# Key norm and output norm of an RWKV-7 group formed per token, two numbers a token, and spread over the channels by products with the unit matrix

## What is computed

```
kk = heads(k * k_k)
kk = kk / max(sqrt(sum(kk * kk, -1)), 1e-12)          # key norm, one number per token and head
...
yc = y - mean(y, -1)
yn = yc * rsqrt(mean(yc * yc, -1) + 64e-5) * g + b    # output norm, one number per token and head
```

## Time and profile before

| | |
|---|---|
| time, median of 3 runs | 4246.4 us (4245.26 to 4247.04) |
| span of the profiled execution | 4199.6 us |
| PE busy, DVE busy, POOL busy | 2858.0, 2419.6, 2387.5 us |
| ACT busy | 671.8 us |
| read from memory over the span | 1310.53 MB, 315 GB/s |

### The profile page before, as it was taken

The page is one execution under the profiler, slowest core; times in us unless marked ns, Lnnn a source line. Parts: engine busy times, 40 slices in busy tenths (PEclk is TensorE's granted clock), DMA queues, the critical chain, the costliest instruction groups (busy, mean ns, idle before and its releaser), DMA issues. The chain is left out here.

```text
span 4199.6 us, 48966 instructions
## 1 busy us (share of the span) xinstructions
PE 2858.0 (68%) x18591; PEld 1580.0 (38%) x18591; DVE 2419.6 (58%) x5633; ACT 671.8 (16%) x1913; POOL 2387.5 (57%) x2194
## 2 busy tenths in 40 slices
PE   7887376787746777768567777667545666675566
PEld 5666354445413343446134343344112222330011
DVE  3427977565864555667855555569745465673311
ACT  3331122220011122101012222101011111000000
POOL 0001366665455665675765665665666776676764
PEclk9988677888977787879788987789767767687788
DMA  3125688889788988899998897998999999999997
GB/s 110 69 67 208 226 303 312 313 332 385 288 324 317 347 289 315 331 374 351 352 371 304 336 339 285 338 374 313 373 378 356 360 383 359 388 373 349 370 365 297
DMA packets 371523, 1325.36 MB, mean 316 GB/s; under 512 B 40188, under 2 KB 75416, under 8 KB 360152
## 3 DMA queue, kind: packets, MB, share of 16 engines
q0 software_dynamic: 314576, 1145.45, 72.7%
q1 hardware_dynamic: 56712, 176.79, 11.2%
HBM read 1310.53 MB, written 11.29 MB: 315 GB/s over the span
## 5 line engine op out<-in xcount | busy, mean ns | idle before, releaser
L752 POOL DMA_INDIRECT ring_u<-in_peer_u,idx x1088 | 1222.6, 1124 | 1088.3 <-DVE gates L1703 396.0
L1460 DVE CUSTOM_DVE_ANT_0 ring_u<-ring_u,h 128x1024 f32<-128x1024 f32 x1088 | 1294.2, 1224 | 568.3 <-DMA ring_u<-in_peer_u,idx 447.3
L752 POOL DMA_INDIRECT ring_v<-in_peer_v,idx_t x1042 | 1114.2, 1069 | 686.5 <-PE pacc L1110 347.9
L1110 PE MATMUL pacc<-ring_v,spread_w 128*32 128x512 f32 x4168 | 1029.2, 737 | 470.6 <-DMA ring_v<-in_peer_v,idx_t 343.0
L1110 PEld LDWEIGHTS pacc<-ring_v,spread_w 128*32 128x32 f32 x4168 | 170.5, 121 | 1050.5 <-DMA ring_v<-in_peer_v,idx_t 686.3
L1085 PE MATMUL pm<-arena 64*64 64x64 f32 (+1 forms) x6256 | 375.8, 257 | 273.8 <-issue 147.1
L1071 PE MATMUL pm<-hT,wts 128*128 128x256 f32 (+2 forms) x2656 | 544.9, 365 | 25.1 <-issue 14.0
L1071 PEld LDWEIGHTS pm<-hT,wts 128*128 128x128 f32 x2656 | 465.0, 208 | 144.6 <-issue 78.0
L1085 PEld LDWEIGHTS pm<-arena 64*64 64x64 f32 x6256 | 295.5, 157 | 434.7 <-issue 251.2
L1071 PE MATMUL pm<-wts,hT 128*128 128x384 f32 (+1 forms) x576 | 201.3, 504 | 7.5 <-DMA wts<-in_sets 7.4
L1071 PE MATMUL pm<-wts,mixT 128*128 128x128 f32 (+1 forms) x1152 | 148.2, 283 | 13.1 <-DVEq L541 5.1
(11 more groups left out here) (223 smaller groups left out, 2708.2 us busy)
## 6 DMA issues: line engine op xcount, KB each, us to landing
wts<-in_sets SPq DMA_DIRECT2D x82, 1536.0 KB
ring_u<-in_peer_u,idx POOLq DMA_INDIRECT x1088
ring_v<-in_peer_v,idx_t POOLq DMA_INDIRECT x1042
wts<-in_sets SPq DMA_DIRECT2D x11, 1024.0 KB
arena<-in_subkeys SPq DMA_DIRECT2D x5, 1024.0 KB
arena<-in_x_prompt SPq DMA_DIRECT2D x8, 512.0 KB
out<-arena SPq DMA_DIRECT2D x64, 64.0 KB
out<-h POOLq DMA_DIRECT2D x8, 512.0 KB
```

The source lines that it names most:

```text
L752: pool.indirect_dma_start(out=out, out_offset=None, in_=table, in_offset=bass.IndirectOffsetOnAxis(ap=index.bitcast(U32), axis=0)).then_in ...
L1110: x = pe.matmul(pacc[out, c, :], spread_w[:, blocks % 2, quad, place % EIGHTH, :], row[:, c * 512:(c + 1) * 512], start=(place == 0), stop ...
L1460: v.tensor_tensor_reduce(ring_u[:, row, :], ring_u[:, row, :], h1[:, g % 4, :], 1.0, 0.0, ALU.mult, ALU.add, dots[:, slot:slot + 1]).then_ ...
```

## The change

For each tile of 128 tokens the squares now are the stationary operand and two columns of `ones2` (or `mean2`) the moving one, so that the sums come out with tokens on the partitions, two numbers for each token (`head_sums`). ACT takes the root and DVE floors and inverts on 128 x 4 numbers. `over_channels` then spreads them back: for each tile and each head one product, with the 128 numbers broadcast to 64 columns as stationary operand and the unit matrix as moving one, into the free half of the same bank. DVE multiplies with that bank in place of the SBUF tile `nrm`. The floor and the inversion of the key norm move from step `grams` to step `decay` on DVE; the spreading stands in step `decay` on PE. The projection `RAW[1]` is cut in two: 5 of its 8 products before the spreading of the output norm, 3 behind it; the barrier signal of PE moves behind the spreading too.

```diff
-        nrm = carve(SEG)
+        inv_k = carve(2 * NT)
+        inv_y = carve(2 * NT)
...
@@ -906,7 +907,7 @@
                         yield "raw"
                         yield "shifted"
                         tl.next(S["n2_full"])
-                        act.activation(nrm[:, 0:w], pm[:, 0, 0:w], ACT.Sqrt).then_inc(S["nrm_ready"], 1)
+                        act.activation(inv_k[0:s.rows, 0:2 * s.tiles], pm[0:s.rows, 0, 0:2 * s.tiles], ACT.Sqrt).then_inc(S["nrm_ready"], 1)
                         tl.next(S["cum_ready"])
                         act.activation(dec_i[:, 0:s.chunks, 1:CH + 1], cum[:, 0:w].rearrange("p (c t) -> p c t", t=CH), ACT.Exp, scale=DECAY)
                         act.activation(dec_n[:, 0:w], cum[:, 0:w], ACT.Exp, scale=-DECAY).then_inc(S["exps"], 1)
@@ -950,7 +951,8 @@
                             yield "state"
                         yield "mean"
                         tl.next(S["var_full"])
-                        act.activation(nrm[:, 0:w], pm[:, 1, 0:w], ACT.Sqrt, bias=eps_gn[:, :]).then_inc(S["ysd"], 1)
+                        act.activation(inv_y[0:s.rows, 0:2 * s.tiles], pm[0:s.rows, 1, 0:2 * s.tiles], ACT.Sqrt,
+                                       bias=eps_gn[0:s.rows, :]).then_inc(S["ysd"], 1)
                         if s.last:
                             tl.next(S["out_full"])
                             act.activation(s_out, pm[:, 0, 0:HD], ACT.Copy).then_inc(S["out_read"], 1)
@@ -1085,6 +1087,20 @@
                     x = pe.matmul(pm[h, bank, col:col + width], lhs[h], rhs[h], start=start, stop=stop, skip_group_check=True)
                 return x
 
+            def head_sums(s, bank, src, heads):
+
+                for t in range(s.tiles):
+                    x = pe.matmul(pm[0:s.rows, bank, 2 * t:2 * t + 2], src[:, sl(s, t)], heads[:, 0:P:HD], start=True, stop=True, skip_group_check=True)
+                return x
+
+            def over_channels(s, bank, inv):
+
+                for t in range(s.tiles):
+                    for i, h in enumerate(halves()):
+                        x = pe.matmul(pm[h, bank, SEG + t * P:SEG + t * P + s.rows], inv[0:s.rows, 2 * t + i:2 * t + i + 1].to_broadcast([s.rows, HD]),
+                                      ident[0:s.rows, 0:s.rows], start=True, stop=True, skip_group_check=True)
+                return x
+
             def keep_block(bank, w, old):
 
                 pe.matmul(pm[:, bank, 0:w], ident[:, :], old.rearrange("p c n -> p (c n)")[:, 0:w], start=True, stop=False,
@@ -1125,11 +1141,16 @@
                             x = pe.matmul(pacc[h, 0, 0:rows], wgt[h, 0:u_slots(g - 1)], ident[h, h], start=True, stop=True, skip_group_check=True)
                     x.then_inc(S["weight_turned"], 1)
 
-            def raw_row(s, j, x, bank):
+            def raw_row(s, j, x, bank, part=None):
 
                 k = set_number("rwkv", s, j)
-                pe.wait_ge(S[f"w{k % 2}"], weights_in(k))
-                dense(pm[:, bank, 0:s.width], lambda n: column(k, x)[:, n, :], lambda n: hT[:, n, 0:s.width]).then_inc(S["raw_full"], 1)
+                if part != 1:
+                    pe.wait_ge(S[f"w{k % 2}"], weights_in(k))
+                steps = range(KT) if part is None else range(5) if part == 0 else range(5, KT)
+                for n in steps:
+                    i = pe.matmul(pm[:, bank, 0:s.width], column(k, x)[:, n, :], hT[:, n, 0:s.width], start=(n == 0), stop=(n == KT - 1))
+                if part != 0:
+                    i.then_inc(S["raw_full"], 1)
 
             def mixing(steps):
                 for kind, s, j in steps:
@@ -1171,11 +1192,12 @@
                         yield "raw"
                         tl.next(S["sq_ready"])
                         tl.next(S["lo_sig"], 3)
-                        pe.matmul(pm[:, 0, 0:w], ones2[:, :], sq[:, 0:w], start=True, stop=True).then_inc(S["n2_full"], 1)
+                        head_sums(s, 0, sq, ones2).then_inc(S["n2_full"], 1)
                         yield "shifted"
+                        tl.next(S["inv_k_ready"])
+                        over_channels(s, 0, inv_k).then_inc(S["inv_k_full"], 1)
                         yield "decay"
                         tl.next(S["kr_ready"])
-                        tl.next(S["nrm_ready"])
                         for c in range(s.chunks):
                             x = per_head(1, c * P, P, bt[:, cols(s, c)], kr[:, c].rearrange("p a t -> p (a t)"))
                         x.then_inc(S["g_full"], 1)
@@ -1255,17 +1277,22 @@
                             raw_row(s, j + 1, *RAW[0])
                         yield "mean"
                         tl.next(S["ysq_ready"])
-                        pe.matmul(pm[:, 1, 0:w], mean2[:, :], sq[:, 0:w], start=True, stop=True).then_inc(S["var_full"], 1)
+                        head_sums(s, 1, sq, mean2).then_inc(S["var_full"], 1)
+                        early = not s.last and j + 1 < NJ
+                        if early:
+                            raw_row(s, j + 1, *RAW[1], part=0)
+                        yield "variance"
+                        tl.next(S["inv_y_ready"])
+                        over_channels(s, 1, inv_y).then_inc(S["inv_y_full"], 1)
                         leave(pe, "pe")
-                        if not s.last and j + 1 < NJ:
-                            raw_row(s, j + 1, *RAW[1])
-                        yield "variance"
+                        if early:
+                            raw_row(s, j + 1, *RAW[1], part=1)
                         if s.last:
                             tl.next(S["out_read"])
                             if j + 1 < NJ:
                                 raw_row(s, j + 1, *RAW[0])
                                 raw_row(s, j + 1, *RAW[1])
-                        tl.next(S["ysd"])
+                        tl.next(S["inv_y_read"])
                         if j + 1 < NJ:
                             raw_row(s, j + 1, *RAW[2])
                         yield "end"
@@ -1526,6 +1553,10 @@
 
                         tl.told(v.tensor_tensor_scan(cum[:, 0:w], restart[:, 0:w], lw[:, 0:w], 0.0, ALU.mult, ALU.add), S["cum_ready"])
                         tl.link(v.memset(dec_i[:, :, 0:1], 1.0))
+                        tl.next(S["nrm_ready"])
+                        norms = inv_k[0:s.rows, 0:2 * s.tiles]
+                        tl.link(v.tensor_scalar(norms, norms, 1e-12, None, ALU.max))
+                        tl.told(v.reciprocal(norms, norms), S["inv_k_ready"])
                         tl.next(S["lo_sig"], 2)
 
                         tl.link(v.tensor_scalar(delta[:, 0:w], a_t[:, 0:w], par[:, KAW + j:KAW + j + 1], one_minus_ka[:, j:j + 1], ALU.mult, ALU.add))
@@ -1533,10 +1564,8 @@
                         tl.link(v.scalar_tensor_tensor(rkk[:, 0:w], K, par[:, RKW + j:RKW + j + 1], R, ALU.mult, ALU.mult))
 
                         yield "decay"
-                        tl.next(S["nrm_ready"])
-                        tl.link(v.tensor_scalar(nrm[:, 0:w], nrm[:, 0:w], 1e-12, None, ALU.max))
-                        tl.link(v.reciprocal(nrm[:, 0:w], nrm[:, 0:w]))
-                        tl.link(v.tensor_tensor(kk[:, 0:w], kk[:, 0:w], nrm[:, 0:w], ALU.mult))
+                        tl.next(S["inv_k_full"])
+                        tl.link(v.tensor_tensor(kk[:, 0:w], kk[:, 0:w], pm[:, 0, SEG:SEG + w], ALU.mult))
                         tl.link(v.scalar_tensor_tensor(sq[:, 0:w], kk[:, 0:w], -1.0, a_t[:, 0:w], ALU.mult, ALU.mult))
                         tl.next(S["exps"])
                         tl.link(v.tensor_tensor(kr[:, 0:s.chunks, 0, :], chunked(kk[:, 0:w]), dec_i[:, 0:s.chunks, 0:CH], ALU.mult))
@@ -1579,8 +1608,11 @@
                         tl.told(v.tensor_tensor(sq[:, 0:w], yraw[:, 0:w], yraw[:, 0:w], ALU.mult), S["ysq_ready"])
                         yield "variance"
                         tl.next(S["ysd"])
-                        tl.link(v.reciprocal(nrm[:, 0:w], nrm[:, 0:w]))
-                        tl.link(v.scalar_tensor_tensor(yraw[:, 0:w], yraw[:, 0:w], par[:, LXG + j:LXG + j + 1], nrm[:, 0:w], ALU.mult, ALU.mult))
+                        spreads = inv_y[0:s.rows, 0:2 * s.tiles]
+                        tl.told(v.reciprocal(spreads, spreads), S["inv_y_ready"])
+                        tl.next(S["inv_y_full"])
+                        tl.told(v.scalar_tensor_tensor(yraw[:, 0:w], yraw[:, 0:w], par[:, LXG + j:LXG + j + 1], pm[:, 1, SEG:SEG + w],
+                                                       ALU.mult, ALU.mult), S["inv_y_read"])
                         tl.link(v.scalar_tensor_tensor(yraw[:, 0:w], yraw[:, 0:w], par[:, LXB + j:LXB + j + 1], bonus[:, 0:w], ALU.add, ALU.add))
                         tl.link(v.tensor_tensor(mixT[:, j, 0:w], yraw[:, 0:w], g_t[:, 0:w], ALU.mult))
                         leave(v, "dve")
```

(2 more changed lines are left out.)

## The result

| | before | after |
|---|---|---|
| median of 9 runs | 4245.3 us (4213.9 to 4278.7) | 4288.9 us (4256.0 to 4316.4) |
| profiled execution: time, span | span 4199.6 us | 4290.1 us, 4288.2 us |
| ratio of times | | 1.009 (1.0064 to 1.0116) |

The change makes the kernel slower, by 38 us by the ratio (4283.5 us) and 44 us by the medians. I had forecast 10 us, with 4284 as the top of the range; the result stands at that edge, outside the 4247 to 4268 that my own account allowed. Ratios and means leave out the six executions, all on the chip of e9 to e12, that ran over 1.5% above the fastest of their kernel; medians are over all.

A forecast was written before the change was run, and what follows sets the result against it. Bounds: a PE, ACT and DVE chain in the opening, full rings stopping gathers in the rounds, near memory's rate at the end. Terms 8.0 + 3.6 - 1.4 = +10.2 us on 4246.4 gave 4256.6 us, range 4230 to 4284.

The forecast's parts named there:

- DVE's saving: Smaller inversions and floor in both norms: DVE loses 3.3 us a unit, 53 us over the 16 wide units.
- The opening: Units 1 to 4: key norm 8 us longer, output norm 3.6 us, together 11.6 us; POOL's first wait 407 to 408.
- That reading PSUM costs DVE nothing: DVE's multiplication reads PSUM in place of SBUF, as L1553 does too; costed at nothing.
- the third rival: New gaps on PE in the opening drop its clock: at most 21 us more, 4278; granted share falls; chance 0.07.
- The key norm in the rounds: DVE's new wait mostly covered; 1.8 us faster behind rows, paying in 5 of 12 units: minus 9 us.
- The output norm in the rounds: Spreading stands behind raw products and v pieces, so DVE's multiplication starts later: plus 5.6 us over three units.
- the three that I named: Units 5, 9 and 11, whose output-norm spreading comes behind five raw products: plus 1.1, 2.3 and 2.2 us.
- PE has 12 x 2.4 = 29 us more to do ... most of that hides in waits for rows, I take 2 us: PE's added work in the 12 units of the rounds, PE busy for 217 of 300 us; counted as 2 us.
- My sign of being wrong: Wrong if POOL's waits for DVE or PE move over 25 us, its first does not grow, or spreading exceeds 2 us.
- Lockstep: In the rounds DVE waits for PE's spreading behind v pieces that wait for gathers: +37 us, 4284; chance 0.11.
- The relief that pays: DVE's saving counts fully in the rounds, 40 us off, less the opening's 11.6: -28 us, 4218; chance 0.19.
- Left outside the span: The 46.8 us between before's profiled span, 4199.6 us, and its median, left as they are in the forecast.

The follow-up runs named there:

- e9: The kernel before itself, unchanged, run again for a trace: 4209.1 us, ratio 1.0035 to before.
- e12: The change with ScalarE's reciprocal square root on its small tiles, PE's spreading waiting for ACT itself: 4224.8 us, 1.0092 of before.
- e5: The change itself, unaltered, on a chip where the kernel before takes 3833 us: 3840.4 us, 1.0019 of before.
- e2: The change for the key norm alone, output norm as before: 3829.7 us, 0.9995 of before.
- e3: The change for the output norm alone, key norm as before: 3842.2 us, 1.0023 of before.
- e10: The change with each small product (sums and spreadings of both norms) issued twice: 4264.9 us, 1.018 of before.
- e1: Before with each inversion, and the key norm's floor, replaced by one cheap operation (results wrong): 3806.2 us, 0.9926 of before.
- e11: Before with both roots replaced by ScalarE's reciprocal square root, so DVE's floor and inversions go: 4193.2 us, 0.9983 of before.
- e6: The change with all of `RAW[1]` behind the spreading of the output norm: 3843.1 us, 1.0016 of before.
- the late place: Key norm's spreading behind `qkv` of tile 1, floor and inverse behind DVE's three operations; added to e6: 3864.6 us, 1.0083 of before.

## Why the forecast was too small

- **DVE's saving** was right: 54.7 us less busy, forecast 53.
- **The opening** was nearly right: POOL's first wait 409.9 us, forecast 407 to 408. In part that is luck, since its parts were off: the spreading takes 0.66 us, near the lower bound and not 1.2; the masking comes 1.5 us later, not 2.0; and in the first unit PE is through with the raw rows 8.5 us behind the output norm's sum, before 7.9, so 0.6 us later and not 1.2. That makes 4 x 1.5 + 3 x 0.6 = 7.8 us; the other 6 us are not accounted for. That reading PSUM costs DVE nothing held: 417 and 480 ns now, 425 and 485 before. The longer opening goes with a lower granted clock. From 110 to 240 us before had 0.89 in its trace and in e9 alike, the change 0.82 here and 0.85 in e5, where the opening was 416.2 us; e2 and e3 had 0.87 and 0.84.

```profile
110.00:240.00 130.00, 115.30 (x1168) 84.52 (x1168) 37.97 (x98) 47.32 (x142) 0.00 (x0) 0.82 0.17 56
```

  So the sign of the third rival came, the falling granted share. The rule of the Trainium skill that I had weighed ("TensorE: Matmul & The Clock Gate", section "Why this matters for your kernels"), that gaps between bursts bring the half speed back, agrees in direction. But e10, with more products in the same places, had 0.89 and an opening of 411.9 us, and e1, with no gap added but on another chip, had 0.87. So the clock's part has no firm size and is not shown.
- **The key norm in the rounds**, forecast -9 us. e2 is even over the whole run with an opening of 404.5 us, and before's opening was 396.0 and 395.5 us in its two traces (on other chips), so there the rounds seem to have given back about 8 us. On the chips at 4200 us nothing shows that they do.
- **The output norm in the rounds**, +5.6 us: e3 costs 10 us in all by the means with an opening of 396.6 us, so about 9 us in the rounds. DVE waits 43.1 us for spreadings in 18 units, 2.4 us each, against 1.6 us saved: a smaller cost a unit than I had, in more units than the three that I named.
- **The step that failed is "PE has 12 x 2.4 = 29 us more to do ... most of that hides in waits for rows, I take 2 us".** The work was even less than counted, 22 us of spreadings in the rounds; that it hides was wrong. e10 doubles them: 30 us more of PE's time there, and 34 us (plus or minus 20) more of the kernel's behind the opening, where my step would have let about 2 through. What the change adds costs 10 us in the rounds on the chips at 3830 us (e5 against e1) and 20 us on that of e9 to e12 (e12 against e11), in place of my 2. The step also left out that PE stands at its queue's head for the two numbers: 31.8 us in the rounds of the trace after, 11.7 of it without a visible cause, 17.0 in e5. That this standing is paid is not shown: e12 has 8.6 us of it in the rounds and no smaller loss. Why PE's time shows, though PE has waits for rows, is argued only: POOL waits for PE to free v rows, 347.9 and 393.3 us in the two traces of before.
- **My sign of being wrong**, POOL's waits moving by more than 25 us, came (43 and 36 us). But the wait for PE moves by 45 us between two traces of before, so that sign could not tell.
- **Lockstep**, the second rival, had the size, 4284 us; how much of its mechanism is there stays open. DVE's waits at the norms did grow (158.7 us against 64.8). e12 took away only PE's wait for DVE; DVE's wait for the spreading was still 101.9 us there. Against DVE's share speaks e6, which has 13.7 us less of it than e5 in the same time; for it speaks the late place, where 60 us of it cost 23 to 25 us.
- **The relief that pays** (4218) is real on the chips at 3830 us, at half its price (e1: 24 us by the means, 5 of them in the opening), and not seen on those at 4200 us.
- **Left outside the span**: the 46.8 us were no constant. Single executions spread over 60 us on the first chip, so the sum should have been put on the median with that as its uncertainty.

Open are: how the 35 to 50 us part between the products, PE's standing and DVE's waits (e12 has 25 us less of PE's standing than the trace after, and no smaller loss that its interval could tell), and why PE stalls on some chips. The products without their hand-overs were not run.

## What to carry to other kernels

Work that is moved to an in-order engine costs its own time, and each hand-over adds a place where one of the two engines stands at the head of its queue; multiply by every use and ask who waits for what is queued behind. Do not write such work down as hidden because the engine is busy for only two thirds: here e10's extra products showed in the time about in full. Read an engine's idle time once, from its products or from its weight loads, not from both. And what a saving on one engine is worth can differ from chip to chip: 28 us here, 12 us or nothing there, with a loss in the opening on both.

## What the runs showed of the hardware that I had not expected

- The same kernel takes 3829 and 3833 us on two chips and 4194 and 4245 us on two others. What goes with it, in all fourteen traces, is 460 to 549 us of PE idle time without a visible cause against 3 to 7 us, up to 23.6 us at a stretch, or as a product every 0.7 to 2.1 us. The transfers of instructions were 147 (before) and 149 packets (the change) on either kind, 0.2 to 0.3% of the DMA engines. The Trainium skill ("Runtime: NRT & Kernel Launch", section "Instruction fetch mechanics") calls the fetch mostly hidden; no run here shows whether these stalls are fetches.
- DVE needs 0.17 to 0.18 us for 128 x 4 numbers, floor or inverse, against 0.29 and 1.75 us for 128 x 256.
- ACT's reciprocal square root of 128 x 256 with a bias took 0.47 us, as the root with a bias (0.47) and more than the root without (0.38). In the key norm it has one table load of 1.28 us, as the root had; in the output norm it has one in each of 20 units, where the root had one in the whole run.
- Within one kernel on one chip, the time went with the mean granted clock: 29 runs of before on the chip of e9 took 4162 to 4233 us with clocks between 0.789 and 0.808, the quicker ones mostly with the higher. The change's mean was 0.005 lower than before's (0.849 against 0.854, on the chip of e5), and e12's as much (0.796 against 0.800 or 0.801); but e9, the same kernel as before, was 0.003 lower. Whether the clock makes these microseconds or the gaps make the clock, no run tells.
